# Splitting the gates of the recurrence: one fp32 product a gate becomes three products of halves, in a one-core Trainium2 kernel

## The reference, cut to what matters

```python
u  = depthwise_conv(xb, p["sconv_w"], p["sconv_b"], SHORT_CONV_PAD)      # 4 taps
gr = einsum("bnkhi,khij->bnkhj", uh, w_r)      # two directions k, 8 heads h, 128x128 each
gi = einsum("bnkhi,khij->bnkhj", uh, w_i)
r, i = sigmoid(gr + b_r), sigmoid(gi + b_i)
log_a = -LRU_C * r * softplus(-lam)
a, bx = exp(log_a), sqrt(-expm1(2.0 * log_a)) * (i * uf)
h_t = a_t * h_{t-1} + bx_t                      # a scan over the tokens
```

## Time and profile before

| | us |
|---|---|
| median of 3 runs | 942.37 |
| lowest, highest of them | 941.29, 944.29 |
| the profiled execution, its own time | 943.91 |
| its span in the profile | 942.1 |
| busy in the span: TensorE / VectorE / ScalarE / GpSimd | 891.3 / 704.2 / 498.2 / 142.5 |
| mean granted TensorE clock, share of full speed | 0.974 |

### The profile page before, as it was taken

One profiled execution on the slowest core, in us unless ns is written; L12 is line 12 of the kernel. 1 busy time (PEld: TensorE's weight loads), 2 busy tenths in 40 slices (PEclk: granted clock), 3 DMA queues, 4 the chain that ended last, 5 costly groups with the idle time before them and its releaser, 6 DMA issues.

```text
span 942.1 us, 17236 instructions
## 1 busy us (share of the span) xinstructions
PE 891.3 (95%) x7064; PEld 833.2 (88%) x7064; DVE 704.2 (75%) x1017; ACT 498.2 (53%) x710; POOL 142.5 (15%) x254
## 2 busy tenths in 40 slices
PE   7999999998997699999999999979999799999995
PEld 5788777688997699989999999979999799999995
DVE  5687578999877599978579985776995876566553
ACT  5374888896544445325553574554534454444441
POOL 0004674710011001400212100300001000000000
PEclk8899999999998799999999999989999799999998
DMA  9935977986575668866628744625566466666661
GB/s 366 359 135 143 311 262 227 294 303 222 174 258 180 218 201 263 297 216 193 185 85 312 269 151 129 213 90 179 161 187 174 142 217 184 187 182 180 201 201 45
DMA packets 56013, 195.43 MB, mean 207 GB/s; under 512 B 7936, under 2 KB 9088, under 8 KB 54528
## 3 DMA queue, kind: packets, MB, share of 16 engines
q1 hardware_dynamic: 40320, 147.73, 49.2%
q0 software_dynamic: 15616, 46.61, 14.4%
HBM read 188.60 MB, written 1.05 MB: 201 GB/s over the span
## 4 chain that ended last, share of the span: by engine, by line
PE 67%; DVE 15%; ACT 7%; DMA 5%; issue 3%; POOL 2%; SPq 0%; DVEq 0%; ACTq 0%; POOLq 0%
PE ps L571 19%; PE ps L572 19%; PE ps L573 19%; DVE w_lo L1336 5%; PE ps L724 3%; ACT w_hi L944 2%; DMA m<-in_mod_w 2%; DMA raw<-in_stream 2%; POOL shifts L459 2%; PE px L644 1%; DMA modw<-in_mod_w 1%; PE ps L655 1%; DVE modw L1370 1%; DVE win L1350 1%; DVE dump L1706 1%
## 5 line engine op out<-in xcount | busy, mean ns | idle before, releaser
L1336 DVE TENSOR_TENSOR w_lo<-raw,w_hi 128x1024 fp32r<-128x1024 f32 x232 | 280.9, 1227 | 120.1 <-ACT w_hi L944 119.6
L944 ACT ACTIVATE w_hi<-raw 128x1024 fp32r<-128x1024 f32 x232 | 243.6, 1056 | 123.5 <-DMA raw<-in_stream 123.3
L571 PE MATMUL ps<-h_hi,w_hi 128*128 128x256 f32 (+1 forms) x928 | 278.5, 300 | 24.7 <-DVE w_lo L1336 13.5
L572 PE MATMUL ps<-h_lo,w_hi 128*128 128x256 f32 (+1 forms) x928 | 273.3, 295 | 0.0
L573 PE MATMUL ps<-h_hi,w_lo 128*128 128x256 f32 (+1 forms) x928 | 273.0, 294 | 0.0
L571 PEld LDWEIGHTS ps<-h_hi,w_hi 128*128 128x128 f32 x928 | 181.4, 195 | 37.2 <-DVE w_lo L1336 18.0
L572 PEld LDWEIGHTS ps<-h_lo,w_hi 128*128 128x128 f32 x928 | 181.5, 196 | 3.7 <-issue 1.2
L573 PEld LDWEIGHTS ps<-h_hi,w_lo 128*128 128x128 f32 x928 | 181.3, 195 | 2.8
L571 PE MATMUL ps<-h2o_hi,w_hi 128*128 128x256 f32 x352 | 102.1, 290 | 0.0
L573 PE MATMUL ps<-h2o_hi,w_lo 128*128 128x256 f32 x352 | 100.0, 284 | 0.0
L572 PE MATMUL ps<-h2o_lo,w_hi 128*128 128x256 f32 x352 | 99.9, 284 | 0.0
(11 more groups left out here) (332 smaller groups left out, 1736.7 us busy)
## 6 DMA issues: line engine op xcount, KB each, us to landing
raw<-in_stream SPq DMA_DIRECT2D x252, 512.0 KB, 3.9
modw<-in_mod_w POOLq DMA_DIRECT2D x80, 512.0 KB, 5.8
m<-in_mod_w SPq DMA_DIRECT2D x8, 1024.0 KB, 19.2
shifts<-upad POOLq DMA_DIRECT2D x128, 35.5 KB, 4.0
c_row<-in_c_rows SPq DMA_DIRECT2D x3, 512.0 KB, 6.1
ctxT<-in_ctxT SPq DMA_DIRECT2D x1, 1024.0 KB, 5.1
x<-in_xT SPq DMA_DIRECT2D x1, 1024.0 KB, 7.1
ctx2T<-in_ctx2T SPq DMA_DIRECT2D x1, 1024.0 KB, 6.6
```

Source lines behind the costliest of these rows:

```text
L571: pe.matmul(o, wh, hi, start=start, stop=False)
L572: pe.matmul(o, wh, lo, start=False, stop=False)
L944: act.activation(w_hi[split[0] % HI_RING][:], raw[n % RING][:], ACT.Copy).then_inc(w_hi_ready, 1)
L1336: v.tensor_tensor(w_lo[n % RING][:], raw[n % RING][:], w_hi[split[0] % HI_RING][:].bitcast(F32), ALU.subtract).then_inc(w_lo_ready, 1)
```

## The change

The gate tiles join the split tiles, and each gate is formed as three fp32r products of halves. The convolved input `u` of a head is split too: ACT rounds it into `u_hi`, DVE writes the rest into `u_lo`. Both have two buffers, used by even and odd heads in turn, in memory that is free until `ga_out` (L1030) writes there. ACT's `u_high(head)` waits until the head two before has been multiplied. Two semaphores are new.

```diff
-SPLIT_NAMES = ("xb", "va", "vg", ...
+SPLIT_NAMES = ("xb", "gate", "va", "vg", ...
+        u_hi = [at(f"u_hi{j}", W + 4 * j, [2, T], F32R) for j in range(2)]
+        u_lo = [at(f"u_lo{j}", W + 4 * j + 2, [2, T], F32R) for j in range(2)]
...
             def gates(head):
                 pair, e = head // 2, head % 2
-                w = weights("gate", pair)
-                pe.wait_ge(u_ready, head + 1)
+                wh, wl = split_weights("gate", pair)
+                pe.wait_ge(u_split, head + 1)
                 for b in range(4):
                     if head:
                         pe.wait_ge(gates_out, 4 * (head - 1) + b + 1)
-                    mm = pe.matmul(px[b][:, :], w[:, 4 * e + b, :], xpad[:, head, :, SCONV_LEFT:SCONV_LEFT + T],
-                                   start=True, stop=True)
+                    mm = three(px[b][:, :], wh[:, 4 * e + b, :], wl[:, 4 * e + b, :], u_hi[e][:], u_lo[e][:], True, True)
                     mm.then_inc(tile_done if e == 1 and b == 3 else gates_pe, 1)
...
+            def u_high(head):
+                act.wait_ge(u_ready, head + 1)
+                if head >= 2 and head % 2:
+                    act.wait_ge(tile_done, TILE[("gate", head // 2 - 1)] + 1)
+                elif head >= 2:
+                    act.wait_ge(gates_pe, 7 * (head // 2 - 1) + 4)
+                act.activation(u_hi[head % 2][:], xpad[:, head, :, SCONV_LEFT:SCONV_LEFT + T], ACT.Copy).then_inc(u_rounded, 1)
...
+            u_high(0)
+            u_high(1)
+            highs("gate", 0)
             vg_out(0)
             sigmoids(0)
+            u_high(2)
             vg_out(1)
             sigmoids(1)
+            u_high(3)
             vg_out(2)
             exps_of(0, ("va", 4))
...
             vg_out(3)
             conv_out(1)
             sigmoids(2)
+            u_high(4)
             vg_out(4)
             sigmoids(3)
+            u_high(5)
             conv_out(2)
             exps_of(1, ("va", 6))
...
             vg_out(5)
             sigmoids(4)
+            u_high(6)
             conv_out(3)
             vg_out(6)
             sigmoids(5)
+            u_high(7)
...
+            def u_low(head):
+                v.wait_ge(u_rounded, head + 1)
+                v.tensor_tensor(u_lo[head % 2][:], xpad[:, head, :, SCONV_LEFT:SCONV_LEFT + T], u_hi[head % 2][:].bitcast(F32),
+                                ALU.subtract).then_inc(u_split, 1)
+
+            u_low(0)
+            u_low(1)
+            lows("gate", 0)
             gated(0)
             lows("va", 2)
             mod_tiles(0, 1)
             gated(1)
             lows("vg", 2)
+            u_low(2)
             mod_tiles(1, 1, 0, 2)
             gated(2)
+            u_low(3)
             lows("vg", 3)
             lru_root(0, ("va", 4))
             mod_tiles(1, 1, 2, 2)
             gated(3)
-            lows("vg", 4)
+            lows("gate", 1)
             lru_scan(0)
             gated(4)
+            u_low(4)
             lows("vg", 5)
             lru_root(1, ("va", 6))
             lows("vg", 6)
             mod_tiles(2, 1, 0, 2)
             gated(5)
+            u_low(5)
             lows("va", 7)
             lru_scan(1)
             gated(6)
+            u_low(6)
             lows("vg", 7)
             mod_tiles(2, 1, 2, 2)
             lru_root(2, ("ga", 0))
             mod_tiles(3, 1, 0, 2)
             lows("ga", 1)
             gated(7)
+            u_low(7)
```

More of the change, by code:

```diff
@@ L98 @@
 PLACE = psum_groups()
-SPLIT_NAMES = ("xb", "va", "vg", "ga", "gb", "ya", "yb", "ou", "og", "oa", "ob", "f", "i", "q", "u", "v", "o", "ga2", "gb2", "pa", "pb", "wo", "ua", "ub",
+SPLIT_NAMES = ("xb", "gate", "va", "vg", "ga", "gb", "ya", "yb", "ou", "og", "oa", "ob", "f", "i", "q", "u", "v", "o", "ga2", "gb2", "pa", "pb", "wo", "ua", "ub",
                "d0", "d1", "d2")
@@ L321, in build @@
         u_ready = sem("u_ready")
+        u_rounded, u_split = sem("u_rounded"), sem("u_split")
         ga_ready = sem("ga_ready")
```

## The result

| | before | after |
|---|---|---|
| median, us | 942.89 (4 runs) | 966.88 (4 runs) |
| lowest to highest | 941.29 to 944.29 | 966.37 to 969.05 |
| the profiled execution, its own time | 943.91 | 966.37 |
| its span | 942.1 | 964.2 |

The changed kernel is slower: after / before is 1.0259, 95% interval 1.0236 to 1.0283. Forecast were 964 us and a range of 954 to 973.

The account below looks back on a forecast made before the run. The stage's end follows VectorE, behind ScalarE's exponentials and TensorE's convolutions. Three stalls, slower clock, cheaper products and splitting make convolve(6) 25.0 late, ya 22 late: 942.4 + 22 = 964.4 us, range 954 to 973.

Parts of the forecast that it names:

- The bound: End of this stage: follows VectorE, which follows ScalarE's exponentials, which follow TensorE's convolutions.
- The products: Gate heads on TensorE: 2.72 us each instead of 3.53, 0.81 less; 6.5 us less over 8 heads.
- rival 5: Gate products on TensorE get no cheaper: 8 x 0.8 back, 968 us; chance 0.17 together with rival 2.
- The start: gates(0) starts 1.0 us later, behind the first halves; two heads give back 1.6, vg 2 ends about 0.5 earlier.
- The three stalls: TensorE ahead of gates(2), (4), (6): idle 7.5, 9 and 8.5 us for a `w_lo` late in VectorE's list.
- rival 2: Longer stalls: `mod_tiles(4)` loads behind `shifted_copies(7)`, or late raw tiles; up to 8 us more, 972; chance 0.17 with rival 5.
- The clock: Behind each of the three stalls: granted clock falls to 0.5, costing 2.0 us more per stall.
- Rival 1: Behind the three stalls: clock stays up, three times 2.0 less, 16 late, 958 us; chance 0.17.
- The work: Extra splitting behind 131 us: 1.5 us more on ScalarE's path and 3.6 us on VectorE's.
- rival 3: No stall at the gates, only splitting work on the path: 3 us late, 945 us; chance 0.06.
- rival 4: No stall, and the stage's end follows TensorE instead of VectorE: 942.4 - 5.5 = 937 us; chance 0.03.

Follow-up runs that it names:

- last kernel: Changed kernel with halves of gates 1 to 3 formed behind the exponentials and TensorE's order changed (va 6, convolve(5), ga 0 moved ahead of gates): 945.48 us, 1.0026 of before.
- work alone: Kernel before plus the splitting work on ScalarE and VectorE, into memory nobody reads, without its waits, gates still fp32: 945.59 us, 1.0021 of before.
- pair with and without needless products: Changed kernel with conv_out(2), (4), (6) waiting for their convolution alone, without and with needless TensorE products in the three waits: 970.32 and 964.21 us.
- light `conv_out`: Changed kernel with conv_out(2), (4), (6) waiting for their convolution alone, no longer rounding the tile four places on first: 970.32 us, 1.0273 of before.
- waits alone: Kernel before plus three TensorE waits at gates(2), (4), (6), no gate split and no product cheaper: 967.87 us, 1.0238 of before.
- light and filled: Changed kernel with conv_out(2), (4), (6) waiting for their convolution alone, plus needless TensorE products in the three waits: 964.21 us, 1.0224 of before.

## Why the prediction was right

**The bound.** Right: the end of the stage follows the lists of VectorE and ScalarE, not TensorE. The last kernel shows it: its TensorE has 5.5 us less to do and no stall at the gates, and yet the stage is 1.1 us longer than before (159.1 against 158.0, last leg set aside) and about as long as with the work alone (159.8).

**The products.** 2.75 to 2.90 us a head at full clock against 2.72 forecast and 3.53 before. Near enough, and worth nothing here: rival 5 is out, and 0.7 a head is saved, not 0.81.

**The start.** 0.97 us of wait at gates(0), 1.0 forecast.

**The three stalls.** 7.40, 10.20 and 8.41 us against 7.5, 9 and 8.5. The cause is shown by taking it away and by bringing it in alone: three waits in the kernel before give a stage of the same length; moving the halves gives back 15 and, with TensorE's order, 21 us. The second stall was 1.2 us longer than forecast. My sum left out the raw tile of va 6, which only rival 2 names in general: the rounding of it stands ahead of `conv_out(2)`, it is loaded into the slot of vg 4 when the late products of vg 4 are done, and it then took 6.3 us to land, not 4.3. `conv_out(2)` was 8.1 late, not 7.4. No run isolates this term: in the kernel with the light `conv_out` the wait is gone, but the rounding moves into the exponentials, and gates(4) starts no earlier.

**The clock.** 0.50 in all three waits; the heads behind them took 1.4, 2.0 and 1.8 us more than 2.84, together 5.2 against the 6.0 forecast, and the pair with and without needless products puts its price on the path at 5 to 6. Rival 1 (the clock stays up) falls. The rule of the Trainium skill, page "TensorE: Matmul & The Clock Gate", section "HAM oscillation — how this bites in real kernels", that a wait for data makes the next work start cold, agrees with the trace here in all three waits.

**The work.** Mis-sized. I put 3.6 us of VectorE on the path, and with ScalarE's 1.5 had 5; the kernel with the work alone has 1.8 us more in the stage. Its extra instructions wait for no raw tile, so 1.8 alone could be too low, but the last kernel, which does the real splitting, agrees (159.1 against 158.0 before, without the extra of the last leg). In the forecast of the changed kernel this did not show, since the stalls hid most of it.

**Rival 2** (transfers late behind the stalls) came true in small. VectorE waited 4.06 us for the load of `mod_tiles(4)` at 213.33, as POOL's queue had `shifted_copies(7)` ahead of it; by my count there was 1 us to spare. The last L1514 was 23.4 late instead of 22, but I put at most 0.5 of that down to this wait: ScalarE's last tanh, which L1514 also needs, was 24.4 late where I had 23.3, and by itself would have held L1514 to 22.9 late. This is an estimate from the rows of both traces.

**The 2.9 us between 964.0 and 966.9.** 1.6 is the stage (23.6 late, not 22). 0.5 is the base, 942.4 from three runs and 942.9 with the fourth. 0.4 is rounding of 964.4, and the other 0.4 is that the medians are 24.0 apart and the stages 23.6. That the sum came so close is partly luck, for its terms were off both ways: the clock 0.8 too dear and the raw tile missing.

Rivals 3 and 4 (no stall) are what the last kernel is, at 945.5: rival 3's 945, and not rival 4's 937.

## What to carry to other kernels

A product that gets cheaper by taking its operands in another form adds a producer, and the producer stands in somebody's queue. Before counting what the product saves, find where in that queue the new operand is made, and what the instruction ahead of it waits for. Here the operand needed 1.2 us of work and came 7 to 10 us late, three times, because it was written down behind an instruction that waited for something else.

In a chain that alternates between engines, as here, a wait costs once for all that follows, and each further wait is added; test it with a kernel that has the wait and nothing else.

## What the runs showed that I had not expected

At short waits the clock may fall or stay. All eleven kernels have a wait of 2.0 to 2.4 us ahead of gb 6. In five profiles (before, changed, waits alone, work alone, light and filled) the last leg behind it took 5.85 or 5.86 us; in the other six 7.11 to 7.35, as the granted clock fell (0.57 to 0.71 over the four microseconds behind the wait). In the kernel before it stayed at full:

```profile
236.00:238.00 2.00, 2.00 (x19) 2.00 (x18) 2.00 (x3) 2.00 (x5) 0.00 (x0) 1.00 0.00 0
```

The same instructions with nearly the same wait thus differ by 1.4 us, 0.15% of the kernel, from one profile to another. It is not only the length of the wait: the last kernel has 1.83 us ahead of the product at 186.70, and the clock fell to 0.53 from 188 to 190, while behind its longer wait of 2.26 us at 161.78 it stayed at 1.00. Each kernel has one profile, so whether it changes between executions of one kernel isn't shown either. What decides it is open. At the longer waits at the gates, from 3.47 us up, it fell each time that TensorE was left without work.
